# Two tiles' experts by streaming both tables instead of the second one only, with the plan of the dense work moved up

## The chip, the cores and the metric

The program runs on one core of a Trainium2 chip, everything in float32. The metric is the device time of one execution in microseconds (us), compared between the kernel before and the kernel after.

## The reference, cut to what matters

One layer of a hybrid model: 1024 prompt tokens and 32 sample tokens, each of width 1024, pass three kinds of attention, gates and an output projection (called dense work below), and then an expert layer in which every token picks 16 of 16384 experts for each of 8 heads:

```python
def _peer(h, wq, subkeys, u, v):
    ...
        q = jnp.einsum("td,de->te", tb, wq).reshape(-1, PEER_HEADS, 2, PEER_HALF)
        sc = jnp.einsum("thjd,hjnd->thjn", q, subkeys).astype(jnp.float32)
        s1, i1 = lax.top_k(sc[:, :, 0], PEER_TOPK)
        s2, i2 = lax.top_k(sc[:, :, 1], PEER_TOPK)
        ...
        best, sel = lax.top_k(cand, PEER_TOPK)
        idx = jnp.take_along_axis(cidx, sel, axis=-1)
        g = jax.nn.softmax(best, axis=-1).astype(tb.dtype)
        ue = jnp.take(u, idx, axis=0)
        ve = jnp.take(v, idx, axis=0)
        a = jax.nn.gelu(jnp.einsum("thkd,td->thk", ue, tb), approximate=False)
        return jnp.einsum("thk,thkd->td", g * a, ve)
```

`u` and `v` are the two expert tables, 16384 rows of 1024 floats (64 MiB) each. An expert's number is 128 i1 + i2.

## The kernel before

**Tiles and runs.** The 1056 tokens are nine tiles of 128 rows (the ninth, number 8, holds the 32 sample tokens). `ORDER` is 0, 1, 8, 2, 3, 4, 5, 6, 7, in three runs of three (`RUNS`, L79). For each run the dense work goes through the stages inputs, attend, merge, out and score (run 0 also memory); score computes the tile's query products and writes the keys' scores to HBM.

**The experts' steps.** A group is one head of one tile (for the sample tile a group holds four heads). There are 66 groups, and each takes 16 steps, one for each chosen expert: 1056 steps, and 44 more for the tail (`STEPS`). In step k

- POOL issues an indirect DMA that gathers 128 rows of `u`, one for each token, 4 KB each, into one of 8 buffers (`gather_u`, L729), and one that gathers rows of `v` for step k - 40 into one of 10 buffers (`gather_v`, L738);
- DVE takes the dot product of the 128 gathered rows with the tokens' rows (L2125, `G_u_rows`);
- ACT takes the gelu of a whole group's 16 dots; DVE multiplies with the softmax weights;
- every fourth step PE adds the four gathered `v` row sets, weighted, to `y_sum` (`weigh_rows`, L2283): eight products 32 x 512, all on a quarter of the array each.

DVE also ranks the next group's scores (`rank`, L2022, in four pieces), one group ahead of its gathers; ACT loads the scores.

**Two tiles by streaming.** For positions 5 and 6 of `ORDER` (tiles 4 and 5, `STREAMED`) `u` is gathered but `v` is not: `by_row` leaves the `v` gathers of 256 steps out, so that steps 584 to 839 gather only `u`. Instead the whole table `v` is read in 128 chunks of 128 rows. A chunk holds the experts with one i1. The weights are first brought into a form that a product can take: for each token a one-hot row over i1 times its weight (`T_hot`, L2337 and L2341) and one over i2 (L2339) are made by DVE for 8 tokens at a time, PE multiplies the two (L2382), which gives for each of 8 tokens a 128 x 64 table of weights, and ACT copies it to `T_spread_w` (L2415). That is called a build; there are 64 (2 tiles x 2 halves of i1 x 16). A chunk is then four products of 128 x 512 (L2395): weights of 2 tiles by halves of 1024 columns, summed over all chunks in the two `scores` buffers of PSUM.

**What sets the order.** All queues are written out by one planner. `plan` (L626) gives for each piece of dense work a number of experts' steps that must stand before it, in proportion to costs in `ticks` (L608), and `weave` (L654) puts dense work and steps of each engine one behind the other accordingly. Engines take their own instructions strictly in that order. For a run its goal is the step at which its scoring is over:

```python
            first = PRELUDE + TOPK * FIRST[sp.place] - 24
            goal = 2 * HEADS + 10 if sp.i == 0 else first + GOAL
```

The streamed work is placed by `stream_at` (L578) at steps after the dense work's end, up to `LAST_CHUNK` = 1046; the loads of chunks (1 MB, two chunks each, two buffers) are on SP's queue (`stream_sp`, L2303). The steps at which the stages start, worked out from `plan`, before and after the change:

| | inputs | attend | merge | out | score | end |
|---|---|---|---|---|---|---|
| run 1 before | 23 | 73 | 186 | 253 | 264 | 354 |
| run 1 after | 23 | 70 | 177 | 240 | 253 | 290 |
| run 2 before | 354 | 407 | 567 | 636 | 648 | 735 |
| run 2 after | 290 | 331 | 456 | 511 | 520 | 607 |

Run 0 ends at step 23 in both. In the trace of before, run 1's dense work spans 617 to 1787 us (scoring from 1485), run 2's 1787 to 3010 (merge from 2546, scoring from 2811), the builds begin at 3010 and the chunks at 3262.

## Time and profile before

| | us |
|---|---|
| runs (3) | 4120.5, 4097.55, 4118.45 |
| median | 4118.45 |
| the profiled execution, device time | 4110.18 |
| its span, first to last instruction | 4108.4 |
| PE busy | 3191.7 |
| mean granted PE clock | 0.836 of full |
| DMA: bytes moved | 1306.97 MB, 318 GB/s |

The profile is one execution. Busy time of PE counts its products; `PEld` is the loading of weights, which goes on beside them. A float32 product is two instructions of the trace (1024 for 512 products of the chunks), a transpose is one. The DMA share is the mean busy share of the core's 16 DMA engines. `x` is a count of instructions; POOL's instructions after the first 550 us are its indirect DMAs. Rows that name a line Lnnn mean the kernel before.

### The profile page before, as it was taken

The numbers are of one execution on the slowest core, as the hardware profiler recorded it, in microseconds if no ns is written. First come the engines' busy times: TensorE is split into PE (matmuls) and PEld (weight loads), VectorE is DVE, ScalarE is ACT, GpSimd is POOL, SyncE is SP. The second block draws the span as 40 slices with busy tenths as digits, with TensorE's granted clock in tenths as the row PEclk, the third lists the DMA queues.
The fourth block names the chain that finished last, engine by engine and source line by source line (L and its number), as shares of the span: only waits on it lengthen the run. The fifth ranks groups of instructions, "written<-read, shape, count | busy, mean of one in ns | idle before, by whom it ended". The sixth has DMA issues, their size and how long they took to land.

```text
span 4108.4 us, 41007 instructions
## 1 busy us (share of the span) xinstructions
PE 3191.7 (78%) x13101; PEld 1812.2 (44%) x13101; DVE 2504.3 (61%) x6368; ACT 917.2 (22%) x1918; POOL 2166.0 (53%) x1892
## 2 busy tenths in 40 slices
PE   8989978867779974668767777986533699888994
PEld 5667554534345432234534444543333533463331
DVE  2133255577766555656478776756999954696542
ACT  1245112244431110112134433211112200121000
POOL 1000034666656547756567766434655566676664
PEclk9999988977779986789877778998755599958996
DMA  6442487999999989989999999877977699989998
GB/s 217 122 148 92 141 291 283 391 335 367 363 342 411 368 340 355 392 320 386 352 337 363 372 349 367 326 264 247 331 274 233 209 401 420 418 288 352 419 420 321
DMA packets 520902, 1306.97 MB, mean 318 GB/s; under 512 B 47120, under 2 KB 243280, under 8 KB 520688
## 3 DMA queue, kind: packets, MB, share of 16 engines
q0 software_dynamic: 267264, 973.20, 62.9%
q1 hardware_dynamic: 213024, 289.45, 20.2%
q10 hardware_dynamic: 40400, 41.70, 3.1%
q8 instruction: 107, 1.75, 0.2%
q14 instruction: 107, 0.88, 0.1%
HBM read 1252.15 MB, written 52.02 MB: 317 GB/s over the span
## 4 chain that ended last, share of the span: by engine, by line
PE 41%; DVE 21%; DMA 15%; issue 9%; DVEq 5%; ACT 3%; POOL 3%; another core or an unknown queue 2%; SPq 1%; ACTq 0%; POOLq 0%
PE scores L889 7%; DVE G_u_rows L2125 7%; DMA G_v_rows<-in_peer_v,G_idxT 7%; PE scores L1773 6%; PE y_sum L2298 5%; PE scores L1777 4%; PE scores L2395 4%; PE scores L1555 3%; PE scores L1967 2%; PE scores L1462 2%; DMA T_chunks<-in_peer_v 2%; PE scores L1862 2%; PE o L1497 2%; POOL G_v_rows L765 1%
## 5 line engine op out<-in xcount | busy, mean ns | idle before, releaser
L765 POOL DMA_INDIRECT G_u_rows<-in_peer_u,G_idx x1056 | 1259.6, 1193 | 960.1 <-DVE G_dots L2125 530.4
L2125 DVE CUSTOM_DVE_ANT_0 G_u_rows<-G_u_rows,G_h 128x1024 f32<-128x1024 f32 x1056 | 1269.1, 1220 | 352.2 <-DMA G_u_rows<-in_peer_u,G_idx 300.7
L765 POOL DMA_INDIRECT G_v_rows<-in_peer_v,G_idxT x800 | 891.7, 1115 | 564.8 <-PE y_sum L2298 325.2
L2298 PE MATMUL y_sum<-G_v_rows,G_zw 128*32 128x512 f32 x3200 | 503.1, 758 | 170.0 <-DMA G_v_rows<-in_peer_v,G_idxT 144.1
L2395 PE MATMUL scores<-T_chunks,T_spread_w 128*128 128x512 f32 x1024 | 466.7, 610 | 26.9 <-DMA T_chunks<-in_peer_v 24.3
L2395 PEld LDWEIGHTS scores<-T_chunks,T_spread_w 128*128 128x128 f32 x1024 | 193.0, 194 | 301.4 <-issue 245.0
L2298 PEld LDWEIGHTS y_sum<-G_v_rows,G_zw 128*32 128x32 f32 x3200 | 100.8, 127 | 444.8 <-issue 440.3
L889 PE MATMUL scores<-A_w_in,A_hT 128*128 128x256 f32 (+2 forms) x864 | 225.8, 422 | 31.1 <-DMA A_w_in<-in_w_in 22.8
L722 POOL MEMSET G_zw<- 128x1024 f32 x2 | 1.9, 964 | 397.1 <-SPq L684 397.1
L889 PEld LDWEIGHTS scores<-A_w_in,A_hT 128*128 128x128 f32 x864 | 171.3, 201 | 85.2 <-DMA A_w_in<-in_w_in 23.3
L1480 PE MATMUL turn<-ident,C_probs 128*128 128x128 f32 x635 | 133.6, 327 | 94.8 <-ACT C_pT L1588 68.8
L1773 PE MATMUL scores<-D_hT,D_w_gate 128*128 128x384 f32 x512 | 172.0, 489 | 0.0
L1480 PEld LDWEIGHTS turn<-ident,C_probs 128*128 128x128 f32 x635 | 86.9, 169 | 192.9 <-ACT C_pT L1588 97.6
L2382 PE MATMUL o<-T_hot 128*128 128x64 f32 x512 | 105.6, 392 | 79.1 <-DVE T_hot L2341 75.2
L2382 PE MATMUL turn<-T_hot 128*128 128x64 f32 x512 | 107.1, 396 | 76.7 <-DVE T_hot L2341 74.3
L1651 DVE TENSOR_REDUCE C_ntop<-scores 128x1 f32<-128x256 f32 (+8 forms) x108 | 66.0, 611 | 127.5 <-PE scores L1462 111.5
L2382 PEld LDWEIGHTS turn<-T_hot 128*128 128x128 f32 x512 | 102.4, 305 | 91.0 <-issue 85.2
L1588 ACT ACTIVATE C_pT<-turn 128x512 f32<-128x512 f32 (+3 forms) x216 | 103.0, 477 | 175.8 <-PE turn L1480 106.6
L1575 ACT ACTIVATE C_probs<-C_probs,C_ntop 128x128 f32<-128x128 f32 (+5 forms) x144 | 104.8, 729 | 166.4 <-DVEq L1649 111.2
L889 PE MATMUL scores<-A_hT,A_w_in 128*128 128x384 f32 x384 | 132.4, 499 | 10.1 <-issue 10.1
L2382 PEld LDWEIGHTS o<-T_hot 128*128 128x128 f32 x512 | 100.7, 301 | 88.8 <-issue 70.5
L1967 PE MATMUL scores<-h2T,F_w_q 128*128 128x384 f32 (+1 forms) x384 | 127.5, 493 | 11.2 <-DMA F_skT<-scratch_skT 11.2
(314 smaller groups left out, 4648.7 us busy)
## 6 DMA issues: line engine op xcount, KB each, us to landing
T_chunks<-in_peer_v SPq DMA_DIRECT2D x64, 1024.0 KB
A_w_in<-in_w_in SPq DMA_DIRECT2D x24, 1024.0 KB
D_w_gate<-in_w_gate SPq DMA_DIRECT2D x24, 1024.0 KB
G_u_rows<-in_peer_u,G_idx POOLq DMA_INDIRECT x1056
G_v_rows<-in_peer_v,G_idxT POOLq DMA_INDIRECT x800
DF_w<-in_w_gate SPq DMA_DIRECT2D x12, 1024.0 KB
DF_w<-in_peer_wq SPq DMA_DIRECT2D x12, 1024.0 KB
F_w_q<-in_peer_wq SPq DMA_DIRECT2D x12, 1024.0 KB
```

Source lines behind the costliest of these rows:

```text
L765: pool.indirect_dma_start(out=buf[:, :], out_offset=None, in_=table, in_offset=bass.IndirectOffsetOnAxis(ap=rows, axis=0)).then_inc(signal ...
L889: last = pe.matmul(self.ps_m[n % 4][:, 0:width], lhs[c], rhs[c], start=(c == 0), stop=(c == len(lhs) - 1))
L1480: last = pe.transpose(ps_t[at % banks][0:w, b - c:b - c + P], probs[:, b:b + w], ident[:, :])
L1555: last = pe.matmul(self.ps_m[1 + 2 * (unit % 2)][:, 0:sp.n], self.D[0]["w_gate"][b][:, c, par * P:(par + 1) * P], hT[:, c, 0:sp.n], start= ...
L1575: act.activation(probs[:, 0:keys], src[:, 0:keys], ACT.Exp, bias=m["ntop"][:, col:col + 1], scale=-1.0 if kind == "diff" else 1.0, accum_o ...
L1773: pe.matmul(gates[:, 0:n], m["w_gate"][b][:, c, block], m["hT"][:, c, :], start=(c == 0), stop=(c == DC - 1))
L1777: last = pe.matmul(branch[:, 0:n], m["w_br"][b][:, c, block], m["oT"][:, 4 * b + c, :], start=(c == 0), stop=(c == 3))
L1967: last = pe.matmul(self.ps_m[k % 2][:, 0:n], w[:, c, j * P:(j + 1) * P], m["h2T"][:, c, :], start=(c == 0), stop=(c == DC - 1))
L2125: dve.tensor_tensor_reduce(out=self.u_rows[slot][:, :], in0=self.u_rows[slot][:, :], in1=self.h2[t % 2][:, :], scale=1.0, scalar=0.0, op0= ...
L2298: last = pe.matmul(self.ps_y[32 * c:32 * (c + 1), cols], self.zw[b % 2][:, lo:lo + 32], self.v_rows[self.ring_v.slot[4 * quad + c]][:, col ...
L2382: last = pe.matmul(bank[:, KEYS_HALF * i:KEYS_HALF * (i + 1)], self.hot2[u % 2][:, i, :], self.hot1[u % 2][:, i, :], start=True, stop=True)
L2395: last = pe.matmul(self.ps_s[s][:, cols], self.spread_w[:, i, P * s:P * (s + 1)], self.chunks[slot][:, c % 2, cols], start=(c == 0), stop= ...
```

## The change

Tiles 4 and 5 (`DENSE`, positions 5 and 6) get no groups of gathers at all. 50 groups and 800 steps are left (`STEPS` = 844), each with its `u` gather and, 40 steps later, its `v` gather. The two tiles' scores are still ranked, as extra groups beside the ordinary ones: 8 of them in steps 272 to 399 and 8 in steps 528 to 655 (`EXTRA`).

Both tables are streamed for them. For each of 128 chunks PE transposes the chunk of `u` (eight 128 x 128 transposes, `turn_u`, in two halves, copied out by ACT), multiplies it with the two tiles' transposed rows `T_pairT` (eight products of 256 columns, `dot_u`), ACT takes the gelu and DVE multiplies with the spread softmax weights (`weight_chunk`), and PE multiplies the result with the chunk of `v` (`sum_v`, four products of 512 columns, as before). The weights are built in three ranges of 43, 43 and 42 values of i1, so 96 builds. The chunks of both tables come as 0.5 MB loads on SP's queue, three buffers for `u` and two for `v`. `plan` gives run 1 a goal of its own (`GOAL_BETWEEN` = 24 in place of 88), and `LAST_CHUNK` is 835.

```diff
-STREAMED = (5, 6)
-HALVES, CHUNKS, TOGETHER, CHUNK_SLOTS = 2, P, 8, 2
-LAST_CHUNK = 1046
+DENSE = (5, 6)
+GATHERED = [at for at in range(TILES) if at not in DENSE]
+GROUP = [(at, ORDER[at], h) for at in GATHERED for h in range(2 if ORDER[at] == SAMPLE else HEADS)]
+EXTRA = {FIRST[3 * (at // 3)] - 1 + h: (at, ORDER[at], h) for at in DENSE for h in range(HEADS)}
+GOAL_BETWEEN = 24
+RANGES = ((0, 43), (43, 86), (86, 128))
+U_CHUNKS, V_CHUNKS = 3, 2
+LAST_CHUNK = 835
...
-            goal = 2 * HEADS + 10 if sp.i == 0 else first + GOAL
+            goal = 2 * HEADS + 10 if sp.i == 0 else first + (GOAL if sp.i == len(SPANS) - 1 else GOAL_BETWEEN)
...
         for k in range(U_SLOTS + V_LAG):
+            if k == FIRST[DENSE[1]] * TOPK:
+                self.enter(pool, len(SPANS) - 1, "merge")
+                pool.iota(self.count, pattern=[[1, P]], base=0, channel_multiplier=0, allow_small_or_imprecise_dtypes=True).then_inc(self.made, 1)
             if k < U_SLOTS:
                 self.gather_u(pool, k)
-            if k >= V_LAG and by_row(k - V_LAG):
-                self.gather_v(pool, v_of(k - V_LAG))
+            if k >= V_LAG:
+                self.gather_v(pool, k - V_LAG)
...
+        for r, (lo, hi) in enumerate(RANGES):
+            late += [("build", s, r, g) for s in range(len(DENSE)) for g in units if r or s]
+            for c in range(lo, hi + 1):
+                if c < hi:
+                    late.append(("turn_u", c, 0))
+                if sums < dots - 1:
+                    late.append(("sum_v", sums))
+                    sums += 1
+                if c < hi:
+                    late.append(("turn_u", c, 1))
+                if c > lo:
+                    late.append(("dot_u", dots))
+                    dots += 1
...
+            if n in EXTRA:
+                r = RANK[EXTRA[n][0], EXTRA[n][2]]
+                if c in (9, 11, 12, 14):
+                    self.rank(dve, r, (9, 11, 12, 14).index(c))
...
+        def load_u(c):
+            slot = c % U_CHUNKS
+            if c >= U_CHUNKS:
+                eng.wait_ge(self.t_turned, self.turn_no["turn_u", c - U_CHUNKS, 1] + 1)
...
+            eng.dma_start(self.u_chunks[slot][:, :], self.a["peer_u"][P * c:P * (c + 1), :]).then_inc(self.t_u[slot], 16)
+
+        def load_v(c):
+            slot = c % V_CHUNKS
+            if c >= V_CHUNKS:
+                eng.wait_ge(self.t_summed, c - V_CHUNKS + 1)
+            eng.dma_start(self.v_chunks[slot][:, :], self.a["peer_v"][P * c:P * (c + 1), :]).then_inc(self.t_v[slot], 16)
...
+        for c in range(CHUNKS + 4):
+            if c - 4 >= V_CHUNKS:
+                load_v(c - 4)
+            if c < CHUNKS:
+                load_u(c)
...
+        elif kind == "turn_u":
+            c, j = at
...
+            for b in range(4):
+                last = pe.transpose(bank[:, P * b:P * (b + 1)], self.u_chunks[slot][:, P * (4 * j + b):P * (4 * j + b + 1)], self.ident[:, :])
+            last.then_inc(self.t_turned, 1)
+        elif kind == "dot_u":
+            c, = at
+            pe.wait_ge(self.t_turn_out, self.turn_no["turn_u", c, 1] + 1)
+            for b in range(DC):
+                last = pe.matmul(bank[:, 0:PAIR], self.uT[c % 2][:, b, :], self.pairT[:, b, :], start=(b == 0), stop=(b == DC - 1))
+            last.then_inc(self.t_dotted, 1)
+        elif kind == "sum_v":
...
+            pe.wait_ge(self.t_weighted, c + 1)
+            pe.wait_ge(self.t_v[slot], 16 * (c // V_CHUNKS + 1))
+            for s in range(len(DENSE)):
+                for cols in (slice(0, D // 2), slice(D // 2, D)):
+                    last = pe.matmul(self.ps_s[s][:, cols], self.gz[c % 2][:, P * s:P * (s + 1)], self.v_chunks[slot][:, cols],
+                                     start=(c == 0), stop=(c == CHUNKS - 1))
...
+    def weight_chunk(self, dve, c):
...
+        dve.wait_ge(self.t_gelued, c + 1)
+        gz = self.gz[c % 2]
+        dve.tensor_tensor(gz[:, :], gz[:, :], self.spread_w[:, c - RANGES[r][0], :], ALU.mult).then_inc(self.t_weighted, 1)
```

Three places of PE's order show what moves. The first is PE in the scoring of run 1: `scores<-h2T` are the query products, `F_qT` the score products, `y_sum` the gathered `v` rows of four steps (eight products a quad). Before:

```order
L1967 MATMUL scores<-h2T,F_w_q_1 128x384 x16
L1978 MATMUL scores<-F_skT_1,F_qT_1 128x128 x6
L2298 MATMUL y_sum<-G_v_rows,G_zw 32x512 x32
L1967 MATMUL scores<-h2T,DF_w 128x384 x16
L1978 MATMUL scores<-DF_w_br,F_qT_0 128x128 x6
L2298 MATMUL y_sum<-G_v_rows,G_zw 32x512 x32
```

and after:

```order
L1996 MATMUL scores<-h2T,DF_w 128x384 x16
L2007 MATMUL scores<-DF_w_br,F_qT_0 128x128 x6
L2338 MATMUL y_sum<-G_v_rows,G_zw 32x512 x8
L1996 MATMUL scores<-h2T,F_w_q_1 128x384 x16
L2007 MATMUL scores<-F_skT_1,F_qT_1 128x128 x6
L2338 MATMUL y_sum<-G_v_rows,G_zw 32x512 x8
```

Between two heads of the scoring stood four quads, 16 steps; now one quad, four steps.

The second is PE in the scoring of run 2, where `h_0` is the last tile's row block of the stage ahead. Before:

```order
L1877 MATMUL turn<-ident,E_h_0 128x128 x4
L1877 MATMUL o<-ident,E_h_0 128x128 x4
L1967 MATMUL scores<-h2T,DF_w 128x384 x16
L1978 MATMUL scores<-DF_w_br,F_qT_0 128x128 x6
L1967 MATMUL scores<-h2T,F_w_q_1 128x384 x16
L1978 MATMUL scores<-F_skT_1,F_qT_1 128x128 x6
```

and after:

```order
L2338 MATMUL y_sum<-G_v_rows,G_zw 32x512 x16
L1996 MATMUL scores<-h2T,DF_w 128x384 x16
L2007 MATMUL scores<-DF_w_br,F_qT_0 128x128 x6
L1996 MATMUL scores<-h2T,F_w_q_1 128x384 x16
L2007 MATMUL scores<-F_skT_1,F_qT_1 128x128 x6
L2338 MATMUL y_sum<-G_v_rows,G_zw 32x512 x32
L1996 MATMUL scores<-h2T,DF_w 128x384 x16
```

Where the stage had no gathered `v` rows, it now has a quad for every four steps.

The third is PE where the builds end and the chunks begin: `T_hot` are builds, `T_chunks` (before) and `T_v_chunk` (after) the products with `v`, `T_u_chunk` the transposes and `T_uT` the dots. Before:

```order
L2382 MATMUL o<-T_hot_1 128x64 x8
L2395 MATMUL scores<-T_chunks,T_spread_w 128x512 x24
L2298 MATMUL y_sum<-G_v_rows,G_zw 32x512 x8
L2395 MATMUL scores<-T_chunks,T_spread_w 128x512 x12
L2298 MATMUL y_sum<-G_v_rows,G_zw 32x512 x8
```

and after:

```order
L2403 MATMUL turn<-T_hot_1 128x43 x8
L2411 MATMUL turn<-ident,T_u_chunk 128x128 x16
L2417 MATMUL o<-T_pairT,T_uT 128x256 x8
L2411 MATMUL turn<-ident,T_u_chunk 128x128 x8
L2417 MATMUL o<-T_pairT,T_uT 128x256 x8
L2411 MATMUL turn<-ident,T_u_chunk 128x128 x4
L2426 MATMUL scores<-T_v_chunk,T_gz 128x512 x4
L2411 MATMUL turn<-ident,T_u_chunk 128x128 x4
L2417 MATMUL o<-T_pairT,T_uT 128x256 x8
L2338 MATMUL y_sum<-G_v_rows,G_zw 32x512 x8
```

A chunk was four products of 512 columns; it is now four of these, eight of 256 columns and eight transposes, and a transposed half always stands between two products.

## Rows read from the trace of the kernel before

**Rows 1.** The page, sections 1 and 2: PE, its clock, DMA share by slice.

```profile
PE 3191.7 (78%) x13101; PEld 1812.2 (44%) x13101; DVE 2504.3 (61%) x6368; ACT 917.2 (22%) x1918; POOL 2166.0 (53%) x1892
...
PEclk9999988977779986789877778998755599958996
DMA  6442487999999989989999999877977699989998
```

**Rows 2.** By stretch, us (x): PE, PEld, DVE, ACT, POOL; clock, DMA share, GB/s.

```profile
617.00:1485.00 868.00, 708.35 (x3051) 389.71 (x3051) 560.21 (x1514) 246.54 (x545) 526.73 (x462) 0.86 0.95 353
1485.00:1787.00 302.00, 169.75 (x705) 76.86 (x706) 177.19 (x437) 30.80 (x58) 212.33 (x183) 0.76 1.00 376
1787.00:2546.00 759.00, 573.54 (x2868) 329.53 (x2868) 517.21 (x1341) 250.61 (x520) 486.11 (x434) 0.81 0.96 356
2546.00:2811.00 265.00, 245.78 (x776) 134.32 (x776) 171.52 (x407) 50.87 (x73) 112.55 (x92) 0.96 0.82 292
2811.00:3010.00 199.00, 114.69 (x352) 70.07 (x352) 162.62 (x417) 26.11 (x46) 118.15 (x89) 0.77 0.85 297
3010.00:3262.00 252.00, 113.11 (x495) 107.58 (x496) 241.02 (x526) 51.72 (x63) 131.44 (x102) 0.50 0.68 226
3600.00:3740.00 140.00, 122.56 (x576) 83.65 (x576) 127.44 (x257) 36.83 (x47) 97.50 (x78) 0.64 0.85 294
3740.00:4020.00 280.00, 253.93 (x800) 98.61 (x798) 136.13 (x321) 17.68 (x32) 178.06 (x161) 0.98 1.03 411
```

**Rows 3.** The page, section 3, DMA queues: packets, MB, share of 16 engines.

```profile
q0 software_dynamic: 267264, 973.20, 62.9%
q1 hardware_dynamic: 213024, 289.45, 20.2%
```

**Rows 4.** Groups by shape (xcount | busy us, mean ns), 3740 to 4020 us.

```profile
L2395 PE MATMUL scores<-T_chunks,T_spread_w 128*128 128x512 f32 x480 | 217.3, 606 | 14.5 <-DMA T_chunks<-in_peer_v 14.4
...
L2298 PE MATMUL y_sum<-G_v_rows,G_zw 128*32 128x512 f32 x320 | 39.0, 605 | 9.7 <-DMA G_v_rows<-in_peer_v,G_idxT 9.5
```

**Rows 5.** Groups by shape, 3010 to 4108 us, DVE.

```profile
L2125 DVE CUSTOM_DVE_ANT_0 G_u_rows<-G_u_rows,G_h 128x1024 f32<-128x1024 f32 x322 | 389.8, 1222 | 274.7 <-DMA G_u_rows<-in_peer_u,G_idx 253.2 <-issue 21.2
...
L2125 DVE DVE_READ_ACCUMULATOR2_ANT G_dots<- 128x1 f32 x322 | 26.6, 82 | 0.0
...
L2339 DVE TENSOR_TENSOR T_hot<-count,T_picksT 128x1024 f32<-128x1024 f32 x64 | 78.1, 1220 | 0.0
L2341 DVE TENSOR_TENSOR T_hot<-T_hot,T_picksT 128x512 f32<-128x512 f32 x64 | 44.3, 693 | 4.7
```

**Rows 6.** Groups by shape, PE, 0 to 550 us.

```profile
L889 PE MATMUL scores<-A_w_in,A_hT 128*128 128x256 f32 x192 | 42.3, 379 | 0.0
```

**Rows 7.** PE in order of time (start us, us), 488 to 492 us.

```profile
489.16 0.60 PE L1877 MATMUL turn<-ident,E_h 128*128 128x128 f32 x4
489.60 0.60 PE L1877 MATMUL o<-ident,E_h 128*128 128x128 f32 x4
```

**Rows 8.** PE in order of time, 11 to 25 us: transposes.

```profile
11.04 1.08 PE L877 MATMUL turn<-ident,A_xn 128*128 128x128 f32 x4 [11.04 <-DVE A_xn L1077]
11.92 1.06 PE L877 MATMUL o<-ident,A_xn 128*128 128x128 f32 x4
```

**Rows 9.** Groups by shape, 3010 to 3262 us: the builds.

```profile
L2382 PE MATMUL turn<-T_hot 128*128 128x64 f32 x249 | 56.9, 423 | 66.6 <-DVE T_hot L2341 64.3 <-ACT T_spread_w L2415 2.3
```

**Rows 10.** Tile T_chunks: duration ns min/median/max, first and last start us.

```profile
L2395 PE MATMUL scores<-T_chunks,T_spread_w x1024: 592/592/1222, 3271.9 to 4014.5; 128*128 128x512 f32 x171
...
L2316 SPq DMA_DIRECT2D out_y<-T_chunks x2: 338/338/338, 4024.8 to 4033.2; - x2
```

**Rows 11.** Groups by shape, ACT, whole span: copies of 512 columns out of PSUM.

```profile
L1588 ACT ACTIVATE C_pT<-turn 128x512 f32<-128x512 f32 x96 | 56.8, 592 | 72.9 <-PE turn L1480 37.5 <-remote 19.8 <-issue 15.5
```

**Rows 12.** DMA issues: KB each, median us from issue to landing.

```profile
E_w_o<-in_w_o SPq DMA_DIRECT2D x18, 512.0 KB, 8.1
```

463 lines of the change are left out of this document (249 added, 214 removed).

## The prediction, made before the changed kernel was run

> **What bounds the kernel now.** The page comes first [rows 1]. PE is busy for 3191.7 us of 4108.4, far more than any other engine, yet 917 us are idle; and the DMA share stands at nine tenths through most slices from 600 us on. Two things compete for the bound, so the span has to be cut into stretches [rows 2]. POOL does nothing there but issue gathers, so its count is the number of gathered row sets. Until 617 us the first run's dense work stands almost alone on PE. From 617 to 2546 us the DMA share is 0.95 to 1.00 while PE has gaps (at its lowest in the scoring of run 1: 169.75 us busy of 302). There the gathers pace the program: every engine passes through the experts' steps in a fixed order, so the dense work placed between two steps waits for them. From 2546 to 2811 us PE is the bound (245.78 of 265) with 0.82 of DMA; in the scoring of run 2 the steps gather only u rows (89 gathers), and DVE (162.62 of 199) is ahead. After 3010 us the builds are DVE's (241.02 of 252), with PE at a clock of 0.50, and from 3740 us PE (253.93 of 280, clock 0.98) and DMA (1.03) are both full.
>
> What a gather costs the DMA engines follows from the queue of the gathers [rows 3]: 62.9% of 4108.4 us is 2584 us, for 1056 + 800 = 1856 gathers, so 1.392 us of all 16 engines each.
>
> **Part 1: the dense part, 617 to 3010 us.** The new plan ends run 1 at step 290 (before 354) and run 2 at step 607 (before 735), as the places of y_sum between PE's rows show. It no longer gathers u for tiles 4 and 5, but from here on every step has its v gather, where before steps 584 to 839 had none. Counted by stretch, with the work of a stretch unchanged and a step's y_sum on PE at 39.0 us / 80 steps = 0.49 us [rows 4]:
> - run 1 up to its scoring: 11 steps fewer, 22 gathers fewer, at most 31 us; part of it is PE's (708 of 868 busy), so I take 868 - 27 = 841.
> - scoring of run 1: 37 steps instead of 90, 106 gathers fewer: 302 - 148 = 154 by DMA; PE keeps 169.75 - 53 x 0.49 = 144. With little room between the two: 165.
> - inputs and attention of run 2: 166 steps instead of 213, 94 gathers fewer: 759 - 131 = 628 by DMA; PE keeps 551, and DVE gains the ranking of the extra groups (below). I take 648.
> - merge and output of run 2: 64 steps, but 128 gathers instead of 92: DMA 0.82 x 265 + 50 = 267; PE 245.78 + 38 x 0.49 = 264. I take 281.
> - scoring of run 2: 87 steps as before, now 174 gathers instead of 89: DMA 0.85 x 199 + 118 = 287, above DVE's 162.62 + 5 extra groups. I take 289.
>
> The sum is 2224 against 2393: 169 us less, dense work over at 617 + 2224 = 2841. From below the DMA bounds this: its busy time in the five stretches is 2242 us, less 101 gathers x 1.392 = 2101, so 2718 at the earliest unless the accounting is off. From above: nothing gained, 3010.
>
> **Part 2: steps 607 to 656.** Fifty steps with two gathers are 139 us of DMA, and some 2.5 MB of first chunks add 7. DVE: a dot costs 1.22 + 0.08 us [rows 5], so 65; ranking costs, from the last stretch of rows 2, (136.13 - 79 x 1.31) / 4.9 groups = 6.6 us a group, so 3.1 own groups and 3 extra ones are 40; a build compares 8 x 43, compares 8 x 128 and multiplies 8 x 43 columns, 0.46 + 1.22 + 0.46 = 2.14 by the rows for 512 and 1024 columns scaled [rows 5], times 16 is 34. Together 140. With both near 145, 155 us: 2996.
>
> **Part 3: the streamed tables, steps 657 to 834, on PE.** Before, a chunk was four products of 512 columns (eight instructions). Now it is that, plus eight transposes, plus eight products of 256 columns (16 instructions):
> - v: 1024 instructions at 217.3 / 480 = 0.453 us [rows 4]: 464, as before.
> - u dots: 2048 instructions at 42.3 / 192 = 0.220 us [rows 6]: 451.
> - transposes: 1024; four of them start 0.44 us after the four before when the clock is at its high level [rows 7]: 113. At the low level it is 0.88 [rows 8].
> - y_sum of the 46 quads of steps left: 46 x 16 x 39.0 / 320 = 90 [rows 4].
>
> That is 1118 us. These group times include the drains that overlap with the next group, which I count as cover for small waits. In range 0, 16 builds in 7 steps are left, and ranges 1 and 2 have 32 each in 14: DVE needs 16 x 2.14 + 7 x 1.7 = 46 and 32 x 2.14 + 14 x 1.7 = 92 each, PE at the low clock 16 x 0.228 = 3.7 us a build at worst [rows 9], 1.8 at the high level. I take 50 + 95 + 95 = 240. Part 3 is 1358 us: 4354. After the last chunk come the x1 load, two norms and the store: before, the last chunk product started at 4014.5 and the last store at 4033.2 [rows 10], so 25 us with its landing. Span 4379, time 4380.
>
> The same sum without stretches: PE loses nothing and gains 451 + 113 us, and 96 builds instead of 64. A build of 43 columns has the same 16 weight loads as one of 64, so 32 more builds are 56 to 117 us. PE busy would be near 3800. The DMA loses 256 gathers x 1.392 = 356 us and gets 67 MB at the hardware queue's 289.45 MB / 830 us [rows 3], 193: it is eased by 163 us. Work leaves a queue that was full for 2400 us and comes to the engine that is needed alone for the last 1500.
>
> **Edits costed at nothing.** The copies of uT, 256 x 0.59 us on ACT [rows 11], lie behind the v product (3.6 us) or the dot (3.5 us) that stands between a transposed half and the next use of its bank. The gelu of a chunk and DVE's multiplication (steps +1 and +2) have a whole iteration of some 7.9 us before the v product asks for them; the instructions queued behind DVE's wait are u dots, whose rows lie ready. A half-MB load lands in 8.1 us [rows 12] and is issued about 12 us ahead. If the cover of both bank waits goes, the copy (0.59) and the end of a quad's last transpose (0.60 - 3 x 0.11 = 0.27) [rows 7] are exposed twice a chunk: 128 x 2 x 0.86 = 220 us. On SP, v and u loads share a queue, each behind a wait on PE, in the order in which PE frees them. The joined semaphores and POOL's late iota (step 544, long after the merge of run 2 opened) cost nothing I can see.
>
> **A rule of the Trainium skill.** The rows show quads of transposes 0.88 us apart in the program's first microseconds [rows 8] and 0.44 us apart right behind products [rows 7]: they do run at 2.4 GHz there. "TensorE: Matmul & The Clock Gate", Part 4 (PE-mode transpose), says that a transpose takes some 275 ns in a kernel and that the clock does not open for transposes as it does for products. By that figure 1024 of them would be 282 us instead of 113, and an estimate from this page would come to 4550. Here they stand between 0.4 us and 3.5 us apart from products, so I go by the rows, and keep the low level as a rival.
>
> **The rivals.**
> - A, not slower: the steps pace the whole dense part, PE's gaps closing with them. Then 2393 x 590/718 = 1966, dense work ends at 2583 and the time is 4122. For it: DMA shares near 1.0 in 1930 us. Against: the last two stretches gain gathers, and 2101 us of DMA cannot fit. It decides only if dense work ends before 2612. Chance 0.05.
> - B: the chunk loop is a chain of waits (both bank waits exposed): 4380 + 220 = 4600. For it: one bank serves all u transposes. Against: the order of PE's rows puts a product of 3.5 us between. 0.10.
> - C: the dense part gains nothing, because attention and merge wait for each other rather than for rows: 4380 + 169 = 4549. That PE is busy for only 573.54 of 759 us there speaks for it, the DMA share against. 0.08.
> - D: the transposes keep the clock low in their part: 4380 + 113 = 4493. 0.05.
> - The forecast, 4380, within 4290 to 4480: 0.72.
>
> **How the numbers follow.** The profiled execution took 4110.18 us, the median of the runs is 4118.45, so I predict the time on the profile's scale, 4380, some 6.4% above the median. The range 4240 to 4550 takes in C and D, and leaves out A, B and a little of both ends. One per cent is what a measurement of this kernel tells from no change; only A and half of its neighbourhood fall under that: faster 0.03, same 0.04, slower 0.93.
>
> **What would show it.** In the new profile dense scoring of run 1 should take about 165 us and that of run 2 about 290; the last transposes of the dense part lie near 2840 us; the chunk loop shows PE above 0.95 at a clock near 1.0, 7.9 us a chunk and a DMA share near 0.6; DVE builds in two blocks of about 95 us. PE is busy near 3800 us. It is wrong if the dense work ends before 2700 or after 3000, or if a chunk costs under 7.3 or over 9 us.

## The result, and the profile of the changed kernel

The changed kernel takes 4508.53 us (median of 4 runs, 4503.85 to 4517.75), the kernel before 4110.49 on the same chip (4 runs, 4097.55 to 4120.5): a ratio of 1.0973, 95% interval 1.0932 to 1.1014. The profiled execution took 4509.32 us with a span of 4507.4, 399 us more than before's 4108.4. The forecast was 4380 with a range of 4240 to 4550. The sign and the range held; the inner band of 4290 to 4480, which was given a chance of 0.72, did not. 128 us of the span are to be explained.

The page, sections 1 and 2, by which [rows 1] is answered:

```profile
PE 3810.2 (85%) x16701; PEld 2396.1 (53%) x16701; DVE 2291.1 (51%) x6048; ACT 1076.6 (24%) x2289; POOL 1754.6 (39%) x1637
...
PEclk9999989777899899877789987765999689977999
DMA  6343679999998989998999889996676467755665
```

PE is busy for 618 us more and DVE for 213 less; the DMA share falls from nine tenths to six at the end. The stretches that answer to [rows 2], each cut where its stage begins (columns: us, then busy us and instructions of PE, PEld, DVE, ACT, POOL; PE's clock, DMA share, GB/s):

```profile
617.00:1497.00 880.00, 704.68 (x3003) 390.72 (x3003) 538.86 (x1461) 242.25 (x538) 484.83 (x441) 0.85 0.93 338
1497.00:1670.00 173.00, 125.16 (x496) 67.39 (x496) 87.86 (x230) 18.58 (x36) 87.33 (x82) 0.87 0.93 342
1670.00:2341.00 671.00, 544.31 (x2669) 328.57 (x2669) 499.29 (x1397) 244.11 (x515) 367.66 (x333) 0.81 0.91 321
2341.00:2630.00 289.00, 270.07 (x962) 139.10 (x966) 147.37 (x347) 48.84 (x79) 135.64 (x125) 0.97 0.92 326
2630.00:2930.00 300.00, 166.90 (x700) 77.59 (x695) 194.54 (x560) 29.68 (x61) 196.20 (x176) 0.76 0.95 356
2930.00:3163.00 233.00, 153.92 (x790) 108.39 (x782) 208.56 (x516) 43.88 (x74) 150.60 (x126) 0.60 0.84 308
3163.00:3517.00 354.00, 351.06 (x1520) 232.41 (x1520) 88.38 (x226) 76.52 (x149) 78.19 (x84) 0.99 0.71 252
3517.00:3637.00 120.00, 110.47 (x577) 99.48 (x576) 91.85 (x155) 27.10 (x38) 29.49 (x27) 0.59 0.37 116
3637.00:3997.00 360.00, 354.94 (x1536) 233.22 (x1536) 94.01 (x238) 79.49 (x150) 80.32 (x85) 1.00 0.72 255
3997.00:4119.00 122.00, 113.98 (x576) 102.90 (x576) 89.86 (x160) 26.38 (x41) 27.58 (x27) 0.56 0.34 108
4119.00:4487.00 368.00, 366.49 (x1604) 234.21 (x1608) 43.78 (x92) 69.92 (x135) 68.75 (x73) 0.99 0.63 223
```

The first five are the dense part, 617 to 2930 us: 2313 us against 2393 before, so 80 us gained where 169 were forecast. Against [rows 2] the five changed by +12, -129, -88, +24 and +101 us, with 21, 101 and 101 gathers fewer and then 33 and 87 more: the price of a gather is not one number. The sixth row holds steps 607 to 656 with the first 16 builds among them and, from 3100 us, the 16 others of the first range. Then chunks and builds take turns: 1082 us of chunks in three ranges, 242 us of builds in two. The last row ends at 4487, and 20 us follow. From the end of the dense work to the end it is 1577 us against 1098 before: 479 us more. The two differences, -80 and +479, are the 399.

The same two stretches as wholes, of the kernel before:

```profile
617.00:3010.00 2393.00, 1812.12 (x7750) 1000.50 (x7750) 1588.75 (x4115) 604.93 (x1240) 1455.87 (x1257) 0.83 0.94 345
...
3010.00:4108.00 1098.00, 831.80 (x3078) 429.50 (x3078) 719.75 (x1596) 142.79 (x203) 662.30 (x573) 0.78 0.90 343
```

and the dense part of the changed kernel:

```profile
617.00:2930.00 2313.00, 1811.12 (x7822) 1003.37 (x7826) 1467.92 (x3992) 583.46 (x1228) 1271.66 (x1154) 0.84 0.92 334
```

PE's busy time in the dense part is the same to 1 us. With 103 gathers fewer (1154 for 1257) it idles 502 us in place of 581. After the dense part PE had 832 busy us before; now the last six rows of the stretches above hold 1451. All of PE's new work stands there.

The chain of waits inside the first chunk range, by line and in order of time (start, us, what):

```profile
by line: PE o L2417 43.2%; PE scores L2426 41.9%; PE turn L2411 11.3%; PE y_sum L2338 4.6%
...
3303.94 0.44 PE turn L2411 x4
3304.37 3.44 PE scores L2426 x8
3307.81 0.44 PE turn L2411 x4
3308.24 3.46 PE o L2417 x16
```

It never leaves PE. A chunk costs 0.44 + 3.44 + 0.44 + 3.46 = 7.78 us (`turn` are the transposes, `scores` the products with `v`, `o` the dots), and no copy, gelu or load stands in between. The gathers, which answer to [rows 3], are 51.0% of 4507.4 us for 1600 of them, 1.437 us each (1.392 before), and POOL waits for buffers:

```profile
L794 POOL DMA_INDIRECT G_u_rows<-in_peer_u,G_idx x800 | 887.2, 1109 | 1172.5 <-DVE G_dots L2154 853.7
L794 POOL DMA_INDIRECT G_v_rows<-in_peer_v,G_idxT x800 | 852.5, 1066 | 1139.2 <-PE y_sum L2338 882.4
...
q0 software_dynamic: 230400, 838.96, 51.0%
```

### The profile page after: what moved, and what is told of

Same layout as the page of the kernel before. It is cut to its first block, busy times and chain, and to the rows that moved or that the text cites. A ratio compares the mean times of both kernels' runs of the same rounds, so it can differ in the third digit from the quotient of the medians.

```text
span 4507.4 us, 48847 instructions
## 1 busy us (share of the span) xinstructions
PE 3810.2 (85%) x16701; PEld 2396.1 (53%) x16701; DVE 2291.1 (51%) x6048; ACT 1076.6 (24%) x2289; POOL 1754.6 (39%) x1637
## 4 chain that ended last, share of the span: by engine, by line
PE 64%; DVE 13%; issue 6%; DMA 6%; DVEq 4%; ACT 3%; another core or an unknown queue 1%; SPq 1%; POOL 1%; ACTq 0%; POOLq 0%
PE o L2417 10%; PE scores L2426 10%; PE scores L918 7%; PE y_sum L2338 6%; PE scores L1802 6%; PE scores L1806 4%; DVE G_u_rows L2154 3%; PE turn L2411 3%; PE scores L1996 3%; PE scores L1584 2%; PE turn L2403 2%; PE o L2403 2%; PE scores L1891 2%; PE scores L1491 2%; PE o L1526 2%
## 5 line engine op out<-in xcount | busy, mean ns | idle before, releaser
L794 POOL DMA_INDIRECT G_u_rows<-in_peer_u,G_idx x800 | 887.2, 1109 | 1172.5 <-DVE G_dots L2154 853.7
L2154 DVE CUSTOM_DVE_ANT_0 G_u_rows<-G_u_rows,G_h 128x1024 f32<-128x1024 f32 x800 | 964.3, 1218 | 43.4 <-issue 25.3
L2417 PE MATMUL o<-T_pairT,T_uT 128*128 128x256 f32 x2048 | 464.3, 380 | 0.0
L2426 PE MATMUL scores<-T_v_chunk,T_gz 128*128 128x512 f32 x1024 | 463.8, 596 | 0.0
L2417 PEld LDWEIGHTS o<-T_pairT,T_uT 128*128 128x128 f32 x2048 | 380.2, 191 | 48.0 <-issue 1.4
L2426 PEld LDWEIGHTS scores<-T_v_chunk,T_gz 128*128 128x128 f32 x1024 | 185.7, 191 | 195.1 <-issue 194.9
L2455 ACT ACTIVATE T_uT<-turn 128x512 f32<-128x512 f32 x256 | 152.8, 597 | 480.7 <-PE turn L2411 398.8
L2403 PE MATMUL o<-T_hot 128*128 128x43 f32 (+1 forms) x768 | 156.9, 391 | 43.4 <-DVE T_hot L2498 33.2
L2403 PE MATMUL turn<-T_hot 128*128 128x43 f32 (+1 forms) x768 | 152.8, 384 | 22.1 <-DVE T_hot L2498 21.0
L2411 PE MATMUL turn<-ident,T_u_chunk 128*128 128x128 f32 x1024 | 157.9, 277 | 10.8 <-ACT T_uT L2455 7.5
```

Source lines behind the costliest of these rows:

```text
L794: pool.indirect_dma_start(out=buf[:, :], out_offset=None, in_=table, in_offset=bass.IndirectOffsetOnAxis(ap=rows, axis=0)).then_inc(signal ...
L2154: dve.tensor_tensor_reduce(out=self.u_rows[slot][:, :], in0=self.u_rows[slot][:, :], in1=self.h2[t % 2][:, :], scale=1.0, scalar=0.0, op0= ...
L2403: last = pe.matmul(bank[:, n * i:n * (i + 1)], self.hot2[u % 2][:, i, :], self.hot1[u % 2][:, i, 0:n], start=True, stop=True)
L2411: last = pe.transpose(bank[:, P * b:P * (b + 1)], self.u_chunks[slot][:, P * (4 * j + b):P * (4 * j + b + 1)], self.ident[:, :])
L2417: last = pe.matmul(bank[:, 0:PAIR], self.uT[c % 2][:, b, :], self.pairT[:, b, :], start=(b == 0), stop=(b == DC - 1))
L2426: last = pe.matmul(self.ps_s[s][:, cols], self.gz[c % 2][:, P * s:P * (s + 1)], self.v_chunks[slot][:, cols], start=(c == 0), stop=(c == C ...
```

## The experiments

Two questions are open: what paces the dense part, since fewer gathers bought less than forecast, and whether the streamed part is PE's products or a chain of waits. In all, 12 kernels ran, on three other chips than the result. The kernel before takes 4039 to 4045 us on them, so each stands as a ratio to the kernel before on its own chip, and differences are taken between ratios and multiplied by 4044. The intervals of the ratios (about 0.002 to each side) make that good to some 10 us. The reference point is the changed kernel run again:

> The changed kernel itself, beside the others of this call, for a comparison on one chip. All theories: ratio to before 1.09 to 1.10.

Measured: 4472.70 against 4044.40, ratio 1.1066 (1.1047 to 1.1084). In the experiments the dense part is taken from 617 us to the last query product, here 2868 us (2910 on the first chip, where the part above was cut at 2930, behind the last score product). Its chunk ranges are 349, 360 and 368 us, its builds 122 and 117:

```profile
617.00:2868.00 2251.00, 1791.79 (x7802) 988.57 (x7802) 1460.73 (x3974) 581.84 (x1227) 1259.08 (x1144) 0.85 0.94 340
```

Five more of the kernels below leave the dense part as it is; in all six the last score product of the dense part starts between 2864 and 2878 us. So a difference of one dense part of under some 15 us says nothing.

**The chunk loop: transposes left out.** From the third chunk on no table chunk is transposed (the dots read the first two chunks' halves), and the load of a `u` chunk, which had waited for a transpose, waits for an earlier dot.

```diff
-                if c < hi:
+                if c < hi and c < 2:
                     late.append(("turn_u", c, 0))
...
-                eng.wait_ge(self.t_turned, self.turn_no["turn_u", c - U_CHUNKS, 1] + 1)
+                if c < U_CHUNKS + 2:
+                    ...
+                else:
+                    eng.wait_ge(self.t_dotted, c - 2)
```

> The changed kernel without the transposes of the u chunks from the third chunk on, and without their copies on ACT: each dot takes the transposed first or second chunk again. 252 of 256 transposed halves go, 1008 transposes. Theory PE-bound loop (the chunk loop is bound by PE's own issue, a quad of transposes 0.44 us apart): 252 x 0.44 = 111 us less, 4508 to 4397. Rival chain of waits (the loop waits for copies and bank turnover): more than the transposes' own time goes, 150 to 330 us, 4180 to 4360. Rival low clock (transposes take PE's clock down around them): 200 us or more less.

Measured: 4419.76, ratio 1.0941 (1.0916 to 1.0966), only 1.25 points or 51 us below the changed kernel; the ranges took 343, 343 and 349 us, 42 less. But PE was not full there any more. The first range, and PE's `v` products in it:

```profile
3126.00:3470.00 344.00, 325.08 (x1182) 200.84 (x1180) 84.59 (x214) 25.47 (x60) 74.81 (x79) 0.96 0.68 245
```

```profile
L2430 PE MATMUL scores<-T_v_chunk,T_gz 128*128 128x512 f32 x328 | 158.9, 630 | 18.4 <-DMA T_v_chunk<-in_peer_v 18.4
```

PE now waits for `v` chunks, which it never did in the changed kernel. The loads of `u` and `v` share SP's queue, so the new wait of the `u` load may come later than the old one and hold the `v` load behind it: the edit would have put a wait of its own in place of the transposes. The next run tests that and sets the wait one chunk earlier:

```diff
-                    eng.wait_ge(self.t_dotted, c - 2)
+                    eng.wait_ge(self.t_dotted, c - 3)
```

> As no_turn (transposes of the u chunks left out from the third on), but with the u loads waiting for the dot of one chunk earlier, so that the v loads behind them on SP's queue go out as early as in the changed kernel. The v products waited for their chunks in no_turn (18.4 us in the first range). Theory PE-bound loop: the loop falls by the transposes' own 108 us (1074 to 966 us in the trace). Rival: the wait stays and the loop stays at 1035, because less time per chunk means that the loads are late by themselves.

Measured: 4347.21, ratio 1.0745 (1.0727 to 1.0763). The ranges took 312, 319 and 328 us:

```profile
3130.00:3442.00 312.00, 312.00 (x1179) 197.98 (x1177) 84.52 (x214) 25.09 (x59) 74.80 (x79) 0.99 0.78 273
3563.00:3882.00 319.00, 319.00 (x1192) 200.26 (x1193) 90.69 (x227) 26.86 (x61) 77.22 (x81) 0.99 0.79 278
4002.00:4330.00 328.00, 328.00 (x1267) 200.44 (x1267) 41.09 (x85) 20.47 (x51) 64.66 (x69) 1.00 0.71 242
```

That is 118 us less than 1077, where 252 quads at 0.44 us are 111; by the ratios the whole program takes 130 us less. PE does not wait in the ranges any more, so the wait of the first edit was the edit's own. The transposes cost about what they occupy at the high level of the clock. Rival B asked for up to 220 us of waits and rival D for 226 us of transposes: both fall.

**The chunk loop: half of each dot.**

```diff
-            for b in range(DC):
+            for b in range(DC // 2):
                 last = pe.matmul(bank[:, 0:PAIR], self.uT[c % 2][:, b, :], self.pairT[:, b, :], ...
```

> The changed kernel with half of each u dot left out: 4 of the 8 products of 256 columns per chunk, 1024 of 2048 PE instructions. Theory PE-bound loop: 1024 x 0.216 = 221 us less, 4508 to 4287. Rival: the loop is bound by the chain through ACT, DVE and the chunk loads, which then shows: 60 to 150 us less only.

Measured: 4245.21, ratio 1.0505 (1.0483 to 1.0527), 227 us below the changed kernel, and 220 in the three ranges (857 us for 1077); 128 x 8 instructions at 0.216 us (3.46 / 16) are 221. The first range shows PE still full after the work shrank, with 274 us for 349:

```profile
3117.00:3391.00 274.00, 273.03 (x1162) 164.29 (x1160) 88.39 (x226) 74.58 (x146) 74.85 (x80) 1.00 0.85 317
```

So in the loop a microsecond of PE is a microsecond of the program, down to 274 us for the first range.

**The dense part: half the bytes.** Every gather fetches 2 KB of a row instead of 4 KB; the other half of each buffer is cleared once.

```diff
-        pool.indirect_dma_start(out=buf[:, :], out_offset=None, in_=table,
+        pool.indirect_dma_start(out=buf[:, 0:D // 2], out_offset=None, in_=table.rearrange("r (h d) -> (r h) d", h=2),
```

> The changed kernel with gathers of half rows (2 KB instead of 4 KB a row, the other half of each buffer holds zeros), same count of gathers, same work on every engine. Theory DMA-paced dense part: the 1164 gathers of the dense part lose 0.7 us each, the dense part falls to what PE allows (1816 us busy at 0.92), from 2313 to about 1970, and the time to about 4150; the chunk part stays at 1540 us within 20. Rival chain of waits between engines in the dense part (DMA is only busy beside it): 0 to 80 us less, 4430 to 4508.

Measured: 4362.93, ratio 1.0799 (1.0774 to 1.0823), 108 us less:

```profile
617.00:2773.00 2156.00, 1767.19 (x7802) 976.50 (x7802) 1460.21 (x3971) 580.47 (x1227) 1274.12 (x1141) 0.88 0.70 217
```

The DMA share falls from 0.94 to 0.70 and the GB/s from 340 to 217, yet the dense part loses only 95 us of 2251. The rival expected 0 to 80 us and the theory of a DMA-paced part 340. PE's waits tell where the 95 us come from (engine, line, waited for: us in total, times, longest us). In the changed kernel they begin with

```profile
PE y_sum L2338 <- DMA G_v_rows<-in_peer_v,G_idxT: 83.0, 12, 17.5
PE scores L1491 <- DVE C_ntop L1675: 59.5, 24, 5.3
...
PE scores L1996 <- DMA F_skT<-scratch_skT: 21.7, 3, 8.7
...
PE scores L1996 <- DMA DF_w_br<-scratch_skT: 20.0, 2, 17.7
...
PE scores L918 <- DMA A_w_in<-in_w_in: 16.7, 2, 12.0
```

and with half the bytes (its lines stand five further on) they are

```profile
PE y_sum L2343 <- DMA G_v_rows<-in_peer_v,G_idxT: 75.5, 12, 15.8
PE scores L1496 <- DVE C_ntop L1680: 60.0, 25, 5.3
...
PE scores L2001 <- DMA DF_w_br<-scratch_skT: 7.5, 1, 7.5
...
PE scores L923 <- DMA A_w_in<-in_w_in: 1.3, 1, 1.3
```

Added up over the whole lists, attention's waits for DVE, ACT and SP (lines 1491 to 1541) are 194.7 us and stay at 194.3. The waits for `v` rows keep 75.5 of 83.0. What goes are PE's waits for other loads, of keys, weights and stored rows: 69.8 us in the changed kernel, 12.0 with half the bytes. By these waits the gathers' bytes hold up the dense work mostly by way of the other loads. In all PE idles 389 us for 459; the other 25 us are PE's own busy time (1767 for 1792), at a clock of 0.88 for 0.85.

**The dense part: no gathers of `v`, and half of DVE's dots.** The first leaves out all 800 `v` gathers (their buffers hold zeros, which `y_sum` adds); the second takes the dots of the steps over 512 of 1024 columns.

```diff
-            if k >= V_LAG:
-                self.gather_v(pool, k - V_LAG)
...
-            pe.wait_ge(self.v_in[self.ring_v.slot[v]], 16 * self.ring_v.use[v])
+            if v < SLOTS_V:
+                pe.wait_ge(self.cleared, SLOTS_V)
```

> The changed kernel without the v gathers (the v buffers hold zeros, PE's products with them stay). It takes away the same bytes as half_rows (420 MB), but also half of the gathers, with their 1.07 us each on POOL, and the wait of PE for them. Theory bytes: dense part 2156 us as in half_rows, down by 95 from 2251. Theory chain of gathers (count and order of the gathers between DVE's dots and PE's y_sum pace it): dense part down by 150 to 300 us. The chunk loop stays within 15 us of 1074.

```diff
-                dve.tensor_tensor_reduce(out=self.u_rows[slot][:, :], in0=self.u_rows[slot][:, :], in1=self.h2[t % 2][:, :],
+                dve.tensor_tensor_reduce(out=self.u_rows[slot][:, 0:D // 2], in0=self.u_rows[slot][:, 0:D // 2], in1=self.h2[t % 2][:, 0:D // 2],
```

> The changed kernel with DVE's dots over 512 of the 1024 columns (half of each dot product left out): 0.53 us less for each of 800 dots; gathers, bytes and PE as they are. Theory DVE in the chain of the dense part: the 590 dots there lose 313 us of DVE, the dense part falls by 80 to 200 us. Theory DMA or PE: under 40 us. The chunk loop stays within 15 us.

Measured: without `v` gathers 4333.22, ratio 1.0717 (1.0687 to 1.0747), 141 us less; with DVE's dots halved 4383.23, ratio 1.084 (1.0822 to 1.0858), 91 us less. Their dense parts:

```profile
617.00:2748.00 2131.00, 1767.68 (x7801) 982.95 (x7802) 1455.63 (x3966) 579.94 (x1227) 674.51 (x581) 0.87 0.68 221
```

```profile
617.00:2793.00 2176.00, 1762.80 (x7800) 974.15 (x7798) 1159.26 (x3986) 581.91 (x1227) 1155.15 (x1150) 0.88 0.96 352
```

With 563 gathers gone the dense part is 120 us shorter, and with 301 us off DVE it is 75 us shorter (2251 - 2176). Both lie between the theories that were set out for them. No single resource returns more than a fraction of what it is relieved of, and PE is 0.80 to 0.83 busy in all of them. With DVE's dots halved the DMA share even rises to 0.96 while the part gets shorter.

One stretch tells the number of gathers from their bytes: the scoring of run 2, where all twelve waits for `v` rows stand. From the last transposes of `h_0` to the last query product it takes 275 us in the changed kernel, 258 with half the bytes, 270 with DVE's dots halved and 226 without `v` gathers. POOL, which issues the gathers, stands here at

```profile
2599.00:2868.00 269.00, 158.00 (x660) 71.71 (x658) 184.04 (x529) 29.28 (x59) 182.51 (x164) 0.77 0.97 366
```

that is 183 us in its gathers, and it waits for other engines for only 40 us of the 269; with half the bytes a gather takes it no less (1.17 and 1.16 us for `u` and `v`, 1.18 and 1.06 before). So in this stretch the number of gathers that POOL has to issue fits better as the pace than their bytes do. It stays argued: spans on POOL are rough, and the run without `v` gathers takes away PE's wait for them too.

**The streamed part started earlier.** The last run of dense work is planned 48 steps (96 gathers) earlier, and the stream with it.

```diff
-            first = PRELUDE + TOPK * FIRST[sp.place] - 24
+            first = PRELUDE + TOPK * FIRST[sp.place] - 24 - (48 if sp.i == len(SPANS) - 1 else 0)
```

> The changed kernel with run 2 planned 48 steps earlier (its dense work ends at step 559 instead of 607) and the second streamed tile's ranking three groups earlier, so that the streamed part starts at step 609 instead of 657. 96 gathers leave the DMA-full dense part for the chunk loop, where the DMA share is 0.7. Theory PE-bound loop with idle DMA: about 96 x 1.4 = 134 us of DMA pace leave the dense part, 90 to 130 us less than the changed kernel, still slower than before. Rival: the dense part is held by PE and its chains, or the loop takes the gathers' time back: 0 to 40 us less.

Measured: 4447.23, ratio 1.0994 (1.0975 to 1.1012), 29 us less, and the last query product at 2843 us, 25 earlier. At 1.4 us a gather 96 of them would have been 134 us. A gather less in the dense part is worth about 0.3 us here. The part from the first transpose of a chunk to the end grew by 13 us, with 25 us more of PE's busy time, since the `y_sum` of those steps came there. The rival was right.

**The plan alone, in both directions.** In the changed kernel run 1 gets its old goal back; in the kernel before it gets the new one.

```diff
-GOAL_BETWEEN = 24
+GOAL_BETWEEN = GOAL
```

> The changed kernel with the old goal for run 1 (88 instead of 24: run 1's scoring ends at step 353 again), the rest as changed; run 2 still ends at step 607. Theory DMA-paced dense part: the same gathers stand before step 607, so what run 1 loses, run 2 gains: within 30 us of the changed kernel. Rival: the dense part waits for its own chains, so the scoring of run 1 grows by 100 us and run 2 cannot give it back: 60 to 130 us more.

```diff
-            goal = 2 * HEADS + 10 if sp.i == 0 else first + GOAL
+            goal = 2 * HEADS + 10 if sp.i == 0 else first + (GOAL if sp.i == len(SPANS) - 1 else 24)
```

> The kernel before with the changed plan for run 1 alone (its scoring ends at step 291 instead of 354), run 2's end at step 735 as it was. Theory DMA-paced: same gathers before step 735, within 30 us of before. Rival chains: run 1's scoring loses 100 us, run 2 takes back less than half, 50 to 100 us less than before, a version that beats both.

Measured: the old goal 4519.43, ratio 1.1178 (1.116 to 1.1197), 45 us slower than the changed kernel, between the two theories. The new goal in the kernel before 4059.61, ratio 1.0041 (1.0026 to 1.0055), 15 us slower than before itself, as the theory of a DMA-paced part had it and against the rival. The scoring of run 1 with the old goal and, in the changed kernel on the same chip, with the new one:

```profile
1472.00:1776.00 304.00, 168.14 (x704) 75.15 (x704) 216.37 (x612) 36.54 (x71) 209.23 (x186) 0.75 1.01 381
```

```profile
1478.00:1652.00 174.00, 125.29 (x501) 67.48 (x498) 88.45 (x231) 18.72 (x38) 88.55 (x82) 0.87 0.93 344
```

104 gathers more are 130 us more, 1.25 us each: here the forecast's price holds. From there to the last query product it is 1138 us with 498 gathers for the old goal and 1216 with 622 for the new one, 0.63 us each. So the old plan loses more in run 1 than it gives back in run 2, and 46 us are left. In the kernel before it comes out nearly even. With the new goal its run 2 starts at 1644 us and takes 1292 us with 727 gathers to its last query product at 2936, where the kernel before takes 1204 us with 606 (on the first chip), and what follows is 1118 and 1117 us long: what run 1 gains is spent in run 2. The plan suits the stream of both tables and is not a gain by itself.

**The builds.** One run leaves DVE's comparison for i2 out in the two later ranges, the other puts a product of 512 columns, whose result is not used, ahead of each build there, to keep PE's clock up.

```diff
-            dve.tensor_tensor(second, self.count.unsqueeze(1)...
+            if r == 0:
+                dve.tensor_tensor(second, self.count.unsqueeze(1)...
```

> The changed kernel without DVE's comparison over i2 (128 x 1024) in the builds of ranges 1 and 2: 64 of 96 instructions of 1.22 us go, 78 us of DVE's work; PE's products stay. Theory builds bound by PE at the low clock (16 x 0.2 us each): the two blocks of builds stay at 120 us each within 10, time 4490 to 4508. Rival builds bound by DVE: 39 us less in each block, time 4430. Mixed (PE's clock rises when DVE no longer holds it up): blocks of 60 to 80 us, time 4410 to 4430.

```diff
+            if at[1]:
+                pe.matmul(bank[:, :], self.ident[:, :], self.g_fin[:, 0:512], start=True, stop=True)
             for i in range(TOGETHER):
```

> The changed kernel with one more product of 512 columns ahead of each of the 64 builds of ranges 1 and 2, into the bank that the build then overwrites; all else the same. It adds 0.86 us of PE work to each build at the high clock. Theory (a build costs 3.75 us because PE runs at its low clock there): the clock rises, a build takes 1.7 + 0.9 us plus what DVE holds back, a block of 32 falls from 118 to 90 to 105 us. Rival (a build is bound by its weight loads at any clock, or by DVE): a block grows by 28 us to 146.

Measured: without the comparison 4446.86, ratio 1.1009 (1.0986 to 1.1032), 23 us less; its two blocks of builds:

```profile
3463.00:3574.00 111.00, 107.07 (x572) 96.91 (x571) 59.13 (x126) 26.99 (x37) 28.36 (x28) 0.60 0.41 127
3935.00:4053.00 118.00, 113.53 (x577) 102.59 (x578) 56.44 (x131) 26.33 (x41) 26.39 (x27) 0.56 0.36 112
```

DVE's busy time falls by 33 us a block, and the blocks go from 122 and 117 to 111 and 118: PE is the bound of a build block and DVE is not. (The other 13 of the 23 us stand outside the blocks, and the edit does not explain them; the dense part, which it does not touch, is some 6 us shorter too.) With the product added the kernel takes 4506.55, ratio 1.1141 (1.1123 to 1.116), 30 us more, and the blocks 134 and 152, of two profiled executions that are 49 us apart:

```profile
3480.00:3614.00 134.00, 124.10 (x640) 93.15 (x640) 92.44 (x156) 27.38 (x38) 31.10 (x28) 0.76 0.35 107
3975.00:4127.00 152.00, 141.81 (x640) 105.90 (x640) 90.31 (x161) 26.12 (x41) 27.41 (x29) 0.66 0.29 90
```

The granted clock rises from 0.58 and 0.61 to 0.76 and 0.66, but not for the whole block. In the first of the two blocks PE reads (start us, us, engine, line, operation):

```profile
3504.29 3.48 PE L2405 MATMUL o<-T_hot 128*128 128x43 f32 x16
3507.57 2.05 PE L2403 MATMUL turn<-G_g_fin,ident 128*128 128x512 f32 x2
3509.41 3.48 PE L2405 MATMUL turn<-T_hot 128*128 128x43 f32 x16
```

A product begins 3.28 us after the build ahead of it, and the next build 1.84 us after the product: here both still run at the low level, 5.12 us for the pair, where builds alone start 3.41 us apart in the changed kernel. Nine such pairs follow each other from 3492 us on, behind a wait of 4.65 us, and the clock does not rise. It rises behind the quad of `y_sum` at 3538 us, and the next pairs take 2.65 us each: 0.76 us saved for each, against 1.71 lost for each at the low level. Neither theory had both halves: the second block took 152 us, more than the rival's 146.

## Why the prediction was right, and where it missed

**The sign, and the reason for it: right.** "Work leaves a queue that was full for 2400 us and comes to the engine that is needed alone for the last 1500." PE is busy for 3810.2 us where near 3800 were forecast, and it is busy for 1451 of the last 1577 us. In the loop, halved dots on PE and left out transposes each gave back their busy time in full.

**Part 1, the dense part: the step that failed.** The forecast was 2224 us and 169 gained; it took 2313 and gained 80. The step at fault is "There the gathers pace the program": each stretch was priced at gathers left out (or added) times 1.392 us, because the DMA share stood at 0.95 to 1.00. By stretch the forecast missed 39 us in run 1 up to its scoring, 8 in the scoring of run 1, 23 in inputs and attention of run 2, 8 in merge and output, 11 in the scoring of run 2. It missed most in the stretches with most dense work. What the runs put in its place: half the bytes return 95 us, no `v` gathers 120, DVE's dots halved 75, 96 gathers moved out 25; the kernel itself got 80 for 103 gathers, 0.8 us each and not 1.4. By stretch a gather cost 1.28 us in the scoring of run 1 and 0.87 in inputs and attention of run 2, and run 1 up to its scoring gained nothing for 21 fewer. The plan turned back says the same on one chip, 1.25 us in the scoring of run 1 and 0.63 from there on. So the price held where little else stands on PE (about 165 us forecast, 173 measured) and failed where there is much dense work. Over the whole part PE is busy for 0.78 of the time, and its waits are spread over attention's turns with DVE and ACT, loads of keys and weights, and the experts' steps. Whether the scoring of run 1 is paced by the bytes of its gathers or by POOL, which waits for other engines for only 12 of 302 us there before the change, no run tells; a right price may have come from the wrong queue. The Trainium skill, "Perfetto Trace Analysis", Identifying the Most-Contended Engine, says that with 16 DMA engines their occupancy is misleading. The traces agree: with half the bytes the share fell from 0.94 to 0.70, and the part by 95 of 2251 us.

Rival C, which let the dense part gain nothing because attention and merge wait for each other, had a part of the mechanism: attention's waits do not change with the bytes (194.7 and 194.3 us). But inputs and attention of run 2 did get 88 us shorter, so the truth stands between C and the forecast (80 of 169). Rival A, the dense part following its gathers in full, is the far end of the same error; the dense work ended at 2930 us and not near 2583.

**Part 2, steps 607 to 656 and 16 builds: nearly right.** 155 us were forecast; 170 passed from 2930 to 3100.

**Part 3, the chunk loop: mechanism right, 36 us too high.** 1118 forecast, 354 + 360 + 368 = 1082 measured, at a clock of 0.99 and PE 0.99 busy; 7.78 us a chunk for 7.9. The dots and `v` products were priced at group times (0.453 and 0.220 us), which hold the drain at the end of each group; as the chain shows they follow each other every 0.430 and 0.216 us. That is 32 us. `y_sum` was counted with 46 quads, 90 us; 35 stand in the ranges, 65 us at 1.85 each, because most of the others fell into the blocks of builds. Against these 57 us stand 10 in which PE idles in the ranges, and about 11 that are not accounted for. The DMA share was to be near 0.6 and is 0.63 to 0.72.

**Part 3, the builds: a term of the sum mis-sized.** 50 + 95 + 95 = 240 forecast, 63 + 120 + 122 = 305 measured. The step that failed is "DVE needs ... 92 each": DVE was named the bound, as in [rows 2] (241.02 of 252), and PE's 16 x 0.228 = 3.7 us "at worst" was set aside. In the changed kernel DVE waits for PE:

```profile
L2495 DVE TENSOR_TENSOR T_hot<-dist,T_picksT 128x344 f32<-128x344 f32 x30 | 15.4, 514 | 28.1 <-PE o L2403 17.6 <-PE turn L2403 10.2
```

Thinner builds (43 columns in place of 64) had cut DVE's share and not PE's, whose 16 weight loads a build remained; and PE does them at the low level for most of the block, `y_sum` too (3.57 us from start to start for the 16 instructions at 3560 us, 1.85 us in the loop):

```profile
3556.94 3.62 PE L2403 MATMUL o<-T_hot 128*128 128x43 f32 x16
3560.49 3.64 PE L2338 MATMUL y_sum<-G_v_rows,G_zw 128*32 128x512 f32 x16
3564.06 2.04 PE L2403 MATMUL turn<-T_hot 128*128 128x43 f32 x16
3565.93 2.08 PE L2403 MATMUL o<-T_hot 128*128 128x43 f32 x16
3568.53 3.61 PE L2403 MATMUL turn<-T_hot 128*128 128x43 f32 x16 [0.52 <-DVE T_hot L2498]
```

Sixteen instructions take 1.87 us from start to start at 3564 and 3.55 at 3556. The block opens at the high level, and after a wait of 4.65 us of PE for ACT it is at the low one. Each of its three later rises stands right behind a quad of `y_sum`, as here; the first two end after two builds, behind waits of 0.52 and 0.62 us, the third leads into the chunks. In the second block the quad at 4071 us is followed by no rise. In all 24 of its 32 builds run at the low level, 3.41 us each, and 8 at the high one. By the rows all 32 at the high level and their four quads would be an estimated 67 us, less than DVE's 92: the bound would then have been DVE, as forecast. So the term went wrong by PE's clock. That DVE was not the bound is shown by the run without the comparison.

**The sum.** +89 (dense part) + 15 (part 2) - 36 (chunks) + 65 (builds) - 5 (tail, 20 for 25) = 128 us: 4379 becomes 4507.

**Edits costed at nothing: right.** Copies, gelu and loads do not appear in the loop's chain; the wait for `T_uT` comes to 7.5 us in the whole program. The first run without transposes showed what the cover on SP's queue is worth: with a load's wait one chunk later PE waits 18.4 us for `v` in the first range.

**The rule on transposes.** In the loop 8 transposes take 0.88 us of each 7.78, 0.11 us each, at a granted clock of 0.99, the high level of 2.4 GHz, and leaving them out returned 118 us. By the 275 ns of the Trainium skill, "TensorE: Matmul & The Clock Gate", Part 4 (PE-mode transpose), an estimate for the 1008 left out would have been 277 us. In the same place the Trainium skill says that the high clock does not engage for transposes. The measurement decides against both for f32 transposes that stand between long products. The figure is near to what one record lasts here (277 ns in the mean), but four of them start 0.11 us apart. Rival D fell with it.

**Still open.** What exactly paces the dense part: four kernels each relieved one resource, none two together, and whether their gains add up was not tried. Whether POOL's issuing of gathers is what the scorings wait for. And why PE's clock is granted 0.56 to 0.61 in the builds, although PE is busy for 0.92 of them, and why it rises behind some quads of `y_sum` and not with a product of 512 columns ahead of each build.

## What to carry to other kernels

Read a full resource as a bound only after asking what would be waited for if it were empty: a DMA share of 0.94 was worth 95 us of 2251 when its bytes were halved, while with PE at 0.99 in a loop each microsecond taken from PE was one of the program. When work is moved from a shared part to a part at the end that one engine bounds, price it there in full, and price the gain in the shared part stretch by stretch, at what a small cut returns there (from nothing to 1.28 us a gather here). When a step gets thinner for one engine, work out the others' time for it again, at the clock that the old rows of that step show.

## What the runs showed of the hardware that was not expected

- Quads of f32 transposes between products run at the high level of the clock: 0.44 us a quad, clock 0.99.
- In blocks of builds the granted clock is 0.56 to 0.61 with PE busy for 110 of 120 us; a product of 512 columns ahead of each build went with 0.76 and 0.66 and cost more than it gave (286 us for 239 in the two blocks). In the first block of either kernel the clock rises behind quads of `y_sum`.
- Halving the bytes of gathers shortened mainly the waits for other loads (69.8 us to 12.0), not those for the gathered rows (83.0 to 75.5).
- Gathers of half the bytes occupy the DMA engines for 0.6 of the time of full ones, not half: 31.9% of 4359.8 us for 1600 gathers is 0.869 us each, against 51.5% of 4464.0 us, 1.437 us each, for rows twice as long.
- Two loads on one queue: a wait that comes one chunk later for the first holds the second, and took the chunk ranges from 959 us to 1035.
